# Dense products moved between the pieces of both memory attentions of a two-layer decoder trunk

## What is computed

```python
def mem_attend(q, mem_k, mem_v, q_g):          # 4 heads of 64, 256 memory tokens
    qh = rms_norm(q.reshape(bsz, t, MEM_HEADS, MEM_HD), q_g)
    s = jnp.einsum("btnd,bmnd->bntm", qh, mem_k) * MEM_HD ** -0.5
    p = jax.nn.softmax(s, axis=-1)
    return jnp.einsum("bntm,bmnd->btnd", p, mem_v).reshape(bsz, t, W_MEM)

# layer 0 (a_layer): o is the RWKV output, 768 wide
mo = mem_attend(mem_q, mem_k, mem_v, mq_g)     # 256 wide
y = jnp.concatenate([o, mo], axis=-1) * jax.nn.silu(gate)
h = h + y @ w_out                              # K = 1024: 6 chunks from o, 2 from mo
# layer 1 (b_layer)
q, mem_q, gate = jnp.split(rms_norm(h, norm_g) @ w_in, [W_DIFF, W_DIFF + W_MEM], axis=-1)
# gate: 8 chunks of 128 columns, 6 for the prompt/sample attention, 2 for mo
```

## Time and profile before

| | us |
|---|---|
| median of 3 runs | 2493.67 (2489.96 to 2497.48) |
| profiled execution, its own time | 2497.91 |
| its span, first to last instruction | 2496.3 |
| mean granted PE clock | 0.938 of full |
| PE busy | 2199.6 (88%) |
| DVE, ACT, POOL busy | 892.4 (36%), 622.9 (25%), 317.9 (13%) |

### The profile page before, as it was taken

The page is one execution under the profiler, slowest core; times in us unless marked ns, Lnnn a source line. Parts: engine busy times, 40 slices in busy tenths (PEclk is TensorE's granted clock), DMA queues, the critical chain, the costliest instruction groups (busy, mean ns, idle before and its releaser), DMA issues. The chain is left out here.

```text
span 2496.3 us, 47130 instructions
## 1 busy us (share of the span) xinstructions
PE 2199.6 (88%) x20794; PEld 1437.5 (58%) x20794; DVE 892.4 (36%) x1735; ACT 622.9 (25%) x1393; POOL 317.9 (13%) x289
## 2 busy tenths in 40 slices
PE   7999999999999999967994999969977788699399
PEld 4586675856758567546442555535656556577243
DVE  3252453624436344232002303240023577344500
ACT  6222223222232222222003112120023466222200
POOL 0000110201102011010001022001100366122000
PEclk9999999999999999976997999989987799899599
DMA  6000000000000000050201112001120000698211
GB/s 239 28 19 19 27 17 13 29 27 27 20 10 29 27 28 12 23 209 1 106 34 55 40 65 104 1 0 42 34 76 1 1 1 1 213 318 282 121 52 38
DMA packets 50847, 148.96 MB, mean 60 GB/s; under 512 B 11427, under 2 KB 20963, under 8 KB 49236
## 3 DMA queue, kind: packets, MB, share of 16 engines
q1 hardware_dynamic: 39284, 100.07, 11.4%
q0 software_dynamic: 11360, 45.88, 5.1%
HBM read 124.14 MB, written 21.79 MB: 58 GB/s over the span
## 5 line engine op out<-in xcount | busy, mean ns | idle before, releaser
L819 PE MATMUL psum<-xT,rw_w 128*128 128x384 f32 (+1 forms) x1152 | 420.0, 493 | 2.8 <-PEq L169 2.8
L1813 PE MATMUL psum<-kvq_w,xT 128*128 128x384 f32 (+1 forms) x864 | 282.6, 489 | 12.8 <-POOL kvq_w L1767 12.8
L819 PEld LDWEIGHTS psum<-xT,rw_w 128*128 128x128 f32 x1152 | 200.3, 190 | 107.4 <-issue 11.2
L1813 PEld LDWEIGHTS psum<-kvq_w,xT 128*128 128x128 f32 (+1 forms) x864 | 158.9, 185 | 134.8 <-issue 22.2
L302 PE MATMUL psum<-xT,gq_w 128*128 128x292 f32 (+2 forms) x480 | 149.5, 475 | 9.8 <-POOL gq_w L1413 9.8
L302 PEld LDWEIGHTS psum<-xT,gq_w 128*128 128x128 f32 x480 | 92.9, 194 | 66.0 <-issue 38.4
L1350 DVE COPY rwkv_sa_sb<-psum 128x64 f32<-128x64 f32 x96 | 21.6, 225 | 264.8 <-PE psum L1027 264.8
L1718 PE MATMUL psum<-xT,yT 128*128 128x512 f32 (+1 forms) x216 | 98.4, 606 | 13.6 <-DMA xT<-in_w_out 13.6
L1161 ACT COPY rwkv_r_sb<-psum 128x64 f32<-128x64 f32 x96 | 20.4, 213 | 339.7 <-PE psum L1012 307.5
L786 POOL DMA_DIRECT2D out<-rwkv_s x6 | 5.7, 944 | 774.2 <-ACT rwkv_out_p L1182 774.2
L1718 PE MATMUL psum<-xT,y_r 128*128 128x512 f32 (+1 forms) x216 | 98.0, 604 | 1.4 <-PEq L169 1.4
(11 more groups left out here) (413 smaller groups left out, 3800.1 us busy)
## 6 DMA issues: line engine op xcount, KB each, us to landing
xT<-in_cache_k SPq DMA_DIRECT2D x64, 384.0 KB, 6.3
samp_vp<-in_cache_v POOLq DMA_DIRECT2D x64, 384.0 KB, 5.0
rw_w<-in_w_in SPq DMA_DIRECT2D x28, 512.0 KB, 3.8
kvq_w<-in_kv_w SPq DMA_DIRECT2D x4, 1536.0 KB, 6.4
gq_w<-in_b_in SPq DMA_DIRECT2D x10, 512.0 KB, 3.7
front_w<-in_mem_w_kv SPq DMA_DIRECT2D x2, 2048.0 KB, 14.6
x_rows<-in_x_p SPq DMA_DIRECT2D x8, 512.0 KB, 14.4
xT<-in_w_out SPq DMA_DIRECT2D x8, 512.0 KB, 10.8
```

Source lines behind the costliest of these rows:

```text
L819: mm = pe.matmul(out, w[:, load % 2, k, :], xT[:, k, a:b], start=(k == 0), stop=(k == KC - 1))
L1813: mm = pe.matmul(bank[0:r, j % 6, 0:W], xT[:, k, n * P:n * P + r], w[:, i % 2, k, :], start=(k == 0), stop=(k == KC - 1))
```

## The change

Two helper classes give `memory_attention` dense work for 28 points of its PE stream: three in each of the 8 tiles (after the next scores, between the two halves of the transposes, after the values) and four in the tail's chain. `FirstSums` (mem0) computes, for each of the 18 (tile, half) sums of layer 0's output projection, the six matmuls over the RWKV chunks, and adds them to `h`; 84 of the 108 matmuls lie in the loop and 4, 5, 9 and 6 in the tail. `PromptGates` (mem1) computes the six gate chunks of the prompt attention, 144 matmuls, all in the loop, six at each point, and multiplies the gains on POOL. Both use PSUM banks 5 and 7 in turn, so the transposes now go in two halves of four through bank 4 alone, and the values through bank 6 alone.

What else moves: the sixth RWKV chunk stays in SBUF (`y_last`) and is not stored and loaded; the stage cst2 is gone, its loads come last in mem0's SP queue; mem0's SP queue begins with half of `w_out`'s six chunks, the first 512 columns of `y_d`, then residual rows. `out0` and `norm1` become one stage, `last_sums_and_norm`: the two remaining matmuls of each sum, with squares, Ln/Exp, scaling and transposes by groups of tiles [8, 0, 1], [2, 3, 4], [5, 6], [7], one group behind. `gq1` keeps four chunks (2 queries, 2 gates) with the norms' products between them. In mem1 the sample keys are loaded after 16 of the 18 gate pieces and the values after all 18, since they overwrite `xT`. `out1` takes its `h` from dead tiles.

The core of the diff:

```diff
+    JOBS = [("q", 0), ("q", 1), ("g", 0), ("s", 0), ("s", 1), ("g", 1)]
...
+class FirstSums:
...
+        self.units = [(half, n) for half in range(2) for n in range(NTILE)]
+        self.parts = [(u, k) for u in range(len(self.units)) for k in range(len(ys))]
+        blocks = 84
+        cuts = [p * blocks // (3 * NT) for p in range(3 * NT + 1)] + [88, 93, 102, len(self.parts)]
...
+        sp.dma_start(self.w[:, 0:nk, 0:512], w_src[:, 0:nk, 0:512]).then_inc(self.w_loaded[0], 16)
+        for part, (a, b) in enumerate(((0, 512), (512, TT))):
+            sp.dma_start(self.y_r[:, :, a:b], self.y_d[:, 0:nk - 1, a:b]).then_inc(self.y_loaded[part], 16)
+            rows_in(2 * part)
+            rows_in(2 * part + 1)
...
+            if k == 0:
+                pe.wait_ge(self.w_loaded[half], 16)
+                pe.wait_ge(self.y_loaded[n >= 4], 16)
+                if u >= 2:
+                    pe.wait_ge(self.added, u - 1)
+            mm = pe.matmul(self.bank[0:r, 5 + 2 * (u % 2), :], self.ys[k][:, n * P:n * P + r],
+                           self.w[:, k, half * 512:(half + 1) * 512], start=(k == 0), stop=(k == len(self.ys) - 1))
...
+class PromptGates:
...
+            if c >= 2:
+                sp.wait_ge(self.unit_mm, 3 * (c - 1))
+            sp.dma_start(self.w[:, c % 2, :, :].rearrange("p k c -> p (k c)"), self.w_d[chunk]).then_inc(self.w_loaded[c % 2], 16)
...
+    def before_keys(self, sp):
+        sp.wait_ge(self.unit_mm, len(self.units) - 2)
...
+            mm = pe.matmul(out, self.w[:, c % 2, k, :], self.xT[:, k, a:b], start=(k == 0), stop=(k == KC - 1))
...
             for n in range(NT):
                 if n + 1 < NT:
                     scores(n + 1)
+                between.pe(pe, 3 * n)
                 pe.wait_ge(w_ready, n + 1)
-                if n >= 1:
-                    pe.wait_ge(pT_ready, n)
-                for i in range(8):
-                    mm = pe.transpose(bank[:, 4 + i // 4, (i % 4) * P:(i % 4 + 1) * P],
-                                      pr[:, n % 2, i // 2, (i % 2) * P:(i % 2 + 1) * P], ident[:, :])
-                mm.then_inc(w_turned, 1)
+                for part in range(2):
+                    if 2 * n + part >= 1:
+                        pe.wait_ge(pT_ready, 2 * n + part)
+                    for i in range(4):
+                        hh = 2 * part + i // 2
+                        mm = pe.transpose(bank[:, 4, i * P:(i + 1) * P], pr[:, n % 2, hh, (i % 2) * P:(i % 2 + 1) * P], ident[:, :])
+                    mm.then_inc(w_turned, 1)
+                    if part == 0:
+                        between.pe(pe, 3 * n + 1)
                 if n >= 1:
                     values(n - 1)
+                between.pe(pe, 3 * n + 2)
             values(NT - 1)
...
+def last_sums_and_norm(nc, name, w, ys, h, xT, bank, ident, h_store):
+    GROUPED = [[NT, 0, 1], [2, 3, 4], [5, 6], [7]]
...
+            products(GROUPED[0])
+            for g in range(1, len(GROUPED)):
+                products(GROUPED[g])
+                turns(GROUPED[g - 1])
+            turns(GROUPED[-1])
...
+            roots(GROUPED[0])
+            for g in range(1, len(GROUPED)):
+                roots(GROUPED[g])
+                out(GROUPED[g - 1])
+            out(GROUPED[-1])
...
+            adds(GROUPED[0])
+            for g in range(1, len(GROUPED)):
+                adds(GROUPED[g])
+                scales(g - 1)
+                out(GROUPED[g - 1])
+            scales(len(GROUPED) - 1)
+            out(GROUPED[-1])
```

More of the change, by code:

```diff
@@ L1403, in _ @@
             for j, c in enumerate(chunks):
[L1404 to L1414, removed]
+                sp.dma_start(w[:, j, :, :].rearrange("p k c -> p (k c)"), w_d[c]).then_inc(w_loaded[j], 16)
@@ L1416, in _ @@
+        @block.gpsimd
+        def _(pool):
+            for j in range(len(chunks)):
+                pool.wait_ge(w_loaded[j], 16)
+                nc.gpsimd.tensor_tensor(w[:, j], w[:, j], bcast(gain.unsqueeze(2), [P, KC, P]), ALU.mult).then_inc(gained, 1)
         @block.tensor
         def _(pe):
[L1418 to L1422, removed]
+            for m, (kind, c) in enumerate(JOBS):
+                if m >= 2:
+                    before, cc = JOBS[m - 2]
+                    pe.wait_ge({"q": q_read, "s": s_read, "g": g_read}[before], cc + 1)
+                if kind == "s":
+                    pe.wait_ge(sq_ready, c + 1)
+                    for a, b in COLS:
+                        b = min(b, TT)
+                        mm = pe.matmul(wide[:, region(m) + a:region(m) + b], const_view(const, "headsum"), sq[:, c, a:b],
+                                       start=True, stop=True)
@@ L1423, in _ @@
                 else:
+                    j = c + 2 * (kind == "g")
                     pe.wait_ge(gained, j + 1)
[L1425 to L1431, removed]
-                    mm = pe.matmul(wide[:, G[j % 2] + a:G[j % 2] + b], const_view(const, "headsum"), sq[:, c, a:b],
-                                   start=True, stop=True)
+                    mm = project(pe, wide, region(m), w[:, j], xT, TT)
@@ L1454, in _ @@
         @block.vector
         def _(dve):
-            for j in range(n_all):
-                dve.wait_ge(ready, j + 1)
-                ps = wide[:, G[j % 2]:G[j % 2] + TT]
-                if j < 2:
-                    dve.wait_ge(sq_ready, j + 1)
-                    nc.vector.tensor_copy(mqT[:, j, :], ps).then_inc(free, 1)
-                else:
-                    dve.wait_ge(act_read, j - 1)
-                    g = gates[j - 2]
-                    nc.vector.scalar_tensor_tensor(out=g, in0=g, scalar=1.0, in1=ps, op0=ALU.add, op1=ALU.mult).then_inc(free, 1)
@@ L1476, in memory_attention @@
+def memory_attention(nc, name, layer, mqT, mkT, mv, cmk, cmv, gates, const, ones, bank, between, scratch=None, ahead=()):
     ident = const_view(const, "ident")
@@ L1607, in _ @@
                 ins.then_inc(pr_ready, 1)
-                if n >= 1:
-                    turned_out(n - 1)
-            turned_out(NT - 1)
+            exps(0)
+            for n in range(NT):
+                if n + 1 < NT:
+                    exps(n + 1)
+                between.act(act, 3 * n)
+                turned_out(n, 0)
+                between.act(act, 3 * n + 1)
+                turned_out(n, 1)
+                between.act(act, 3 * n + 2)
             for b in range(B):
@@ L2430, in build @@
         ones = sb("ones", [P, P])
-        load_tensors(nc, "cst2", [(late[:, :], i["const2"]), (rows2[:, :], i["rows2"].partition_broadcast(P))], [(ones[:, :], 1.0)])
         h_d = nc.dram_tensor("residual", (TT, D), F32).ap()
```

371 lines of the change are left out of this document (291 added, 80 removed).

## The result

The changed kernel takes 2410.43 us (median of 4 runs, 2407.70 to 2412.64) against 2493.05 for the kernel before in the same session: ratio 0.9667, 95% interval 0.9649 to 0.9685, or 83 us less. The forecast was 75 us less. The profiled execution has a span of 2411.0 us at a mean clock of 0.953 (before 2496.3 and 0.938).

What follows compares the result with a forecast made beforehand. PE was taken to bound the kernel, with time lost to idling and 1.2 GHz around the memory attentions. Layer 0 -47.8 and layer 1 -27.6 sum to -75.4 us, from 2493.7 to 2418; range 2404 to 2444.

Steps and rivals of the forecast that it cites:

- What bounds the kernel: Whole kernel: PE sets the end; time to be won is where PE idles or runs at 1.2 GHz.
- Between the stages: Between rwkv and mem0: 11.0 us without PE work become a barrier of 1.1 us, -9.9.
- mem0's start: Start of mem0: first sum at 10.5 us, after weights and y load, then 3.0 us lost to low clock.
- Its loop: mem0's loop: 98.8 us of PE work plus 1.6 of waits, ending at 113.9 us, was 65.4.
- chains-bind rival: DVE and ACT chains in the 16 tiles: each tile waits 2 us more, +32, giving 2450 us; chance 15%.
- Its tail: mem0's tail: 14.1 us for keys plus 35.7, so mem0 ends at 163.7, was 97.0: +66.7.
- The out stage: out0 and norm1 merged: 54.8 us against 159.4, -104.6.
- gq1: Layer 1's gate and query stage with four chunks: 80.1 us against 167.6, -87.5.
- mem1: Layer 1's memory attention: loop end 124.0, tail 33.6, so 157.6 us against 97.7, +59.9.
- The clock that does not hold: Merged loops: clock falls as in the old loops, gain gone at 2493 us; chance 3% slower, 2% near no change.
- break-even: Merged loops: at a mean clock of 0.74 they take 75 us more, 2493 us; below that the change is slower.
- The loads don't bind: Judges the rival that loads bind: first sum at 20 us, mem1's keys and chunk 5 late, +20, 2438 us; chance 8%.

Runs made afterwards that it cites:

- e3: Changed kernel with all dense products of each attention in one block at the first of the 28 points; 2510.01 us, ratio 1.0053 to the kernel before.
- e2: Layer 1's part of the change alone, layer 0 as in the kernel before; 2467.00 us, ratio 0.9876 to the kernel before.
- e5: Changed kernel with each tile's dense products all at the tile's first point; 2425.59 us, ratio 0.9707 to the kernel before.
- e4: Changed kernel with the out stage's four groups made one, DVE scaling and copying in turn; 2405.13 us, ratio 0.9632 to the kernel before.
- e7: Changed kernel with 16 of the 144 gate products moved from mem1's loop to its tail; 2418.93 us (median of three), ratio 0.9689 to the kernel before.

## Why the prediction was right, step by step

**What bounds the kernel.** Right: the time was in the two attentions, as idle PE and low clock, and e3 shows that putting the work in those places is what counts. I had said that the idle time is the room into which matmuls fit, and counted the clock as a condition. It was nearly as large a term as the idle time (19.3 and 20.0 against 25.1 and 25.1 us in the two loops of e3).

**Between the stages.** -9.8 for -9.9. The barrier is there, the 11 us are gone. The rwkv stage itself ended 3.6 us earlier than before, which I had not in the sum; by the starts listed at e2 it can't be told from scatter.

**mem0's start.** The first sum began 11.0 us after the stage's, predicted 10.5, and of it PE waited 7.6 for `y_r`. A low clock of 0.65 followed, as said. The 2.3 us that I took as fixed in a load are shown by no row; what the trace has is 10.5 us from the issue of the first part of y (1.31 MB) to its landing.

**Its loop.** It ended 113.7 us after the stage's start, predicted 113.9. Two terms were off by little and against each other: the 1.6 us of waits for `w_ready` did not come (no such row in the trace), and the start was 0.5 later. The chains-bind rival is out: no wait of PE for DVE or ACT stands in either loop, and DVE has 29.9 us of work in 98.2.

**Its tail.** Predicted 35.7 us after the keys, measured 31.1: the largest miss. Two terms make 4.0 of the 4.6. The values I took from the earlier trace rows, 7.01 us, at the clock that the tail had before; with 24 dense products in it the tail had 0.87, and they took 4.39 us. The transposes and the products with ones, 3.1 in the sum, took 1.7 (0.38, 0.59 and 0.70):

```profile
1224.00 0.70 PE L1675 MATMUL psum<-mem_red,ones 128*128 128x256 f32 x2 [1.38 <-DVE mem_red L1779]
...
1229.83 4.39 PE L1685 MATMUL psum<-mem_ps,mem_vn 128*64 128x8 f32 x128
```

The bracket in the first line is the wait behind the adds on DVE: 1.38 us for 1.6 predicted. The low start of the dense products was right as well: 3.0 us predicted, and the first four matmuls (eight records) took 6.48 where 3.4 is the rule.

```profile
1203.48 6.48 PE L1461 MATMUL psum<-xT,y_r 128*128 128x512 f32 x8
```

I had priced that start and then left the products behind it at the low clock. The miss is not scatter: from the end of the key scores to the out stage the two executions of the changed kernel took 32.2 and 32.0 us; their 2.1 us lie in the key scores, where I had 14.1 for the whole part, and they had 14.3 and 16.5.

**The out stage.** 55.7 for 54.8, and by the reasons given: PE waits twice 2.3 us for ACT's copy, which stands behind the roots of the next group (predicted 2.2), and 6.8 in all for DVE's scaling:

```profile
1264.28 1.94 PE L1846 MATMUL psum<-base,out_scaled 128*128 128x128 f32 x8 [2.31 <-ACT xT L1872]
```

**gq1.** 76.3 for 80.1. Three terms were each a little large: the start 5.5 for 6.3, the first chunk 16.6 for 17.9, the end after the last product 5.8 for 7.3. In the last one I counted the load of the table for Exp behind the wait for the products; ACT had done it at 1687.5, before that wait ended. Together 3.6 of the 3.8.

**mem1.** Loop end 121.7 for 124.0, tail with barrier 34.1 for 33.6. The one wait of the loop is 1.9 us for POOL's first gain; the keys and chunk 5 were covered as said.

**The rivals.** The clock that does not hold: out, 1.00 in both loops. It would not have been out for any place of the work: with the same products as one block the bare loops have 0.69 and 0.67 (e3), and that kernel is slower than before. (The 0.74 that I gave as the break-even is a mean over loops with the dense work in them, and is not to be set against these two.) With one dense piece of 9 to 11 us in every tile (e5) it held. The loads don't bind either: the first sum came after 11.0 us and not 20, and there is no wait for the keys or chunk 5.

The Trainium skill (TensorE: Matmul & The Clock Gate, A second HAM failure mode: psum-queue depth-cycling) has the clock oscillate where a kernel cycles through PSUM banks with short idles. The changed kernel doesn't test that: its loops change banks every few us, but PE hardly idles in them (97.91 us busy of 98.20). e5 tests a part of it: with eight idles of 0.7 us in each loop the clock stayed at 1.00. The bare loops, with idles of 2.9 us, had 0.67 to 0.74, and no run here shows whether the bank changes have a part in that.

The Trainium skill (same page, Part 4: PE-mode transpose) also says that the full clock does not engage for transposes. The trace disagrees: four of them took 0.60 us throughout the loop, eight 1.09 in the keys, the 2.4 GHz figure of the earlier trace rows.

**Total.** 75.4 predicted, 83 measured. Layer 0 is 3.7 us better than said (51.5 for 47.8 by the stages), layer 1 5.6 (33.2 for 27.6). In layer 0 it is the tail's products that I priced at the low clock of the kernel before; in layer 1 gq1's start, first chunk and end, and the start of mem1's loop (its first sum at 5.7 us for 6.3, and a smaller loss at low clock than the 3.2), each a microsecond or two large. The stages ahead of both add 3.6, likely scatter, and those behind take 2.9 back; by the spans the difference is 85.3, by the medians 83.

## What to carry to other kernels

Where an engine idles for the latency of a chain and its clock is low, there are two gains in placing dense work between the steps, the idle time and the clock of what was there already; price both, from the rows, and price what stands behind the new work at the new clock. The place matters more than the merging: the same products as a block ahead of the loop gave all of it back (e3). Cover each wait of the chain with a piece of its own, but before a piece goes to a later place look at which loads wait for it, since they overwrite its inputs, and at which loads it covers where it stands.

## What the runs showed of the hardware

- A stretch in which PE counts as busy three quarters of the time can be at 1.2 GHz for most of it: mem1's tail has PE busy 25.9 of 35.5 us at 0.64, directly behind 111 us at 1.00; mem0's tail, the same code with 24 dense products in it, has 0.87.
- The clock of one stretch is not the same from one execution to the next, even for the same code: 64 records of 128x16 took between 8.88 us (e4) and 11.71 (e7) in the nine executions that have mem0's merged loop ahead of it.
- The 128 records of 8 columns took 3.90 to 4.90 us in mem0's tail behind dense products, and 7.00 us in mem1's tail and 7.01 in e3, which have none in the tail.
- The load of an activation table is done ahead of the semaphore wait of the activation that needs it, when ACT is idle (gq1: load at 1687.5 us, the wait over at 1700.9), so it costs nothing there; in the out stage two loads of 1.28 us stand in each of the four groups, between the last square and the Exp.
